# Six query and key chunks turned by VectorE and DMA instead of TensorE, in a float32 two-block transformer kernel

## The reference

```python
h = _rms_norm(x, attn_norm[l])
proj = h @ w_in                        # [256, 2048] @ [2048, 5664]
qf, kf, vf, ff, qn, kc, vc, ks, vs, kw, vw, gt = jnp.split(proj, cuts, axis=-1)
qf = _rms_norm(qf.reshape(B, T, Hf, Dh), fox_q_norm)      # 8 heads of 128
kf = _rms_norm(kf.reshape(B, T, Hf, Dh), fox_k_norm)      # 8 heads
qn = _rms_norm(qn.reshape(B, T, G, R, Dh), nsa_q_norm)    # 8 heads
# then: attention with a forget gate over qf, kf, vf (8 heads); compressed, selected and
# windowed attention over qn, kc/vc, ks/vs, kw/vw (8 heads, 2 groups); output projection;
# SwiGLU FFN.  The second block: adaLN, attention and a causal convolution, FFN.
```

## Time and profile before

| | |
|---|---|
| median of 3 runs | 2233.22 us (2232.3 to 2233.9) |
| the profiled execution | 2231.85 us |
| its span in the profile | 2230.1 us |
| TensorE (matmuls) busy | 2208.2 us, 99% |
| VectorE, ScalarE, GpSimd busy | 71%, 49%, 10% |
| DMA | 518.06 MB, mean 232 GB/s |

### The profile page before, as it was taken

One profiled execution on the slowest core, in us unless ns is written; L12 is line 12 of the kernel. 1 busy time (PEld: TensorE's weight loads), 2 busy tenths in 40 slices (PEclk: granted clock), 3 DMA queues, 4 the chain that ended last, 5 costly groups with the idle time before them and its releaser, 6 DMA issues.

```text
span 2230.1 us, 29184 instructions
## 1 busy us (share of the span) xinstructions
PE 2208.2 (99%) x10077; PEld 1826.6 (82%) x10077; DVE 1586.5 (71%) x2041; ACT 1096.5 (49%) x1536; POOL 232.5 (10%) x214
## 2 busy tenths in 40 slices
PE   9999999999999999999999999999999999999998
PEld 7888878888888888888888887788888888888886
DVE  7546678877777778877866888997887545554555
ACT  6556574544434444344455776654444344443444
POOL 5003001000000000000001887000010000000000
PEclk9999999999999999999999999999999999999999
DMA  8556628788888888888856664767997666666664
GB/s 293 169 183 190 195 76 309 263 290 284 285 288 288 285 282 283 289 289 281 272 163 194 192 182 130 260 247 244 307 294 252 196 200 203 202 191 195 199 203 146
DMA packets 310569, 518.06 MB, mean 232 GB/s; under 512 B 55320, under 2 KB 63896, under 8 KB 310192
## 3 DMA queue, kind: packets, MB, share of 16 engines
q1 hardware_dynamic: 306032, 515.73, 71.3%
q10 hardware_dynamic: 4416, 0.79, 0.2%
HBM read 510.15 MB, written 2.10 MB: 230 GB/s over the span
## 4 chain that ended last, share of the span: by engine, by line
PE 94%; DVE 2%; ACT 2%; issue 1%; DMA 1%; SPq 0%; DVEq 0%; ACTq 0%
PE bank L1111 31%; PE bank L1127 29%; PE bank L1128 29%; PE bank L1179 1%; PE bank L1096 1%; DVE w_both L2170 1%; PE bank L1082 1%; PE bank L1212 0%; ACT prob_mid L1653 0%; PE bank L1246 0%; PE bank L1200 0%; DMA raw<-in_w_in 0%; ACT w_both L1604 0%; DMA x_res<-in_x 0%; PE bank L1003 0%
## 5 line engine op out<-in xcount | busy, mean ns | idle before, releaser
L2170 DVE TENSOR_TENSOR w_both<-raw,w_both 128x1024 fp32r<-128x1024 f32 x763 | 950.8, 1250 | 520.2 <-ACT w_both L1604 508.4
L1604 ACT ACTIVATE w_both<-raw 128x1024 fp32r<-128x1024 f32 x763 | 806.4, 1060 | 969.1 <-PE bank L1111 920.4
L1127 PE MATMUL bank<-w_both,act_hi 128*128 128x512 f32 x1984 | 775.6, 391 | 1.7 <-ACT w_both L1604 1.7
L1128 PE MATMUL bank<-w_both,act_lo 128*128 128x512 f32 x1984 | 772.3, 389 | 0.0
L1111 PE MATMUL bank<-w_both,act_hi 128*128 128x512 f32 x2168 | 578.0, 390 | 1.1 <-ACT w_both L1604 0.6
L1111 PEld LDWEIGHTS bank<-w_both,act_hi 128*128 128x128 f32 x2168 | 405.7, 188 | 86.6 <-issue 1.8
L1127 PEld LDWEIGHTS bank<-w_both,act_hi 128*128 128x128 f32 x1984 | 372.5, 188 | 78.6 <-ACT w_both L1604 2.1
L1128 PEld LDWEIGHTS bank<-w_both,act_lo 128*128 128x128 f32 x1984 | 372.5, 188 | 76.1
L1127 PE MATMUL bank<-w_both,mid_hi 128*128 128x512 f32 x960 | 375.8, 391 | 1.1 <-DVE mid_lo L2081 0.4
L1128 PE MATMUL bank<-w_both,mid_lo 128*128 128x512 f32 x960 | 373.7, 389 | 0.0
L2128 DVE SCALAR_TENSOR_TENSOR ada_acc<-ada_raw,c_act,ada_acc 128x512 f32<-128x512 f32 x360 | 269.8, 749 | 10.9 <-DMA ada_raw<-in_ada_w 3.8
(11 more groups left out here) (315 smaller groups left out, 1027.9 us busy)
## 6 DMA issues: line engine op xcount, KB each, us to landing
ada_raw<-in_ada_w SPq DMA_DIRECT2D x192, 512.0 KB, 5.3
raw<-in_w_gate SPq DMA_DIRECT2D x176, 512.0 KB, 4.6
raw<-in_w_up SPq DMA_DIRECT2D x176, 512.0 KB, 4.8
raw<-in_w_down SPq DMA_DIRECT2D x176, 512.0 KB, 4.3
raw<-in_w_in SPq DMA_DIRECT2D x167, 512.0 KB, 3.6
raw<-in_w_out SPq DMA_DIRECT2D x60, 512.0 KB, 5.4
h_tok<-h_blk SPq DMA_DIRECT2D x128, 32.0 KB, 3.9
x_res<-in_x SPq DMA_DIRECT2D x8, 256.0 KB, 5.6
```

Source lines behind the costliest of these rows:

```text
L1127: pe.matmul(A_[t][:, :], h_, w_hi[:, s, kk, :], start=(k == 0), stop=False)
L1128: pe.matmul(A_[t][:, :], l_, w_hi[:, s, kk, :], start=False, stop=False)
L1604: act.activation(w_hi[:, U % SPLIT_SLOTS].rearrange("p k n -> p (k n)"), raw_of(c, u).rearrange("p k n -> p (k n)"), ACT.Copy).then_inc(hi ...
L2170: dve.tensor_tensor(w_lo[:, U % SPLIT_SLOTS].rearrange("p k n -> p (k n)"), raw_of(c, u).rearrange("p k n -> p (k n)"), w_hi[:, U % SPLIT_ ...
```

## The change

For six chunks (fq 0, fq 4, fk 0, fk 4, nq 0, nq 4) TensorE's transposes go. In their place:

- VectorE (`cut_heads`) turns `ysb` in 32x32 squares, two instructions of 128x512, in unit 3 of the next chunk behind `pre`. In chunks 1 and 7 (behind fq 0 and nq 0) it does so in unit 5. It counts `heads_cut` and `turned`.
- SyncE (`move_heads`) moves the squares with 16 DMAs of 32 KB, in four groups of four: the first behind the load of unit 7 of that chunk, after a wait for the cut, the others behind the loads of units 0, 1 and 2 of the chunk after. Each counts `heads_moved`.
- ScalarE and VectorE do `post` in unit 2 of the chunk after, not at the end of the chunk, and wait for `heads_moved`. They read the moved tile in SBUF and not the PSUM bank.

The tiles for squares lie over memory that is used at other times. The core of the diff:

```diff
+    CUT_TURNS = [("normed", "fq", 0), ("normed", "fq", 4), ("normed", "fk", 0), ("normed", "fk", 4),
+                  ("normed", "nq", 0), ("normed", "nq", 4)]
+    MOVED_IN = {c["C"] + 1: c["prev"] for c in S_IN1 + S_IN2 if c["prev"] in CUT_TURNS}
...
+            def move_heads(prev, a):
+
+                n, i = CUT_TURNS.index(prev), TURNS.index(prev)
+                blk, tok = squares_of(prev)
+                if a == 0:
+                    sp.wait_ge(heads_cut, n + 1)
+                    sp.wait_ge(turned, i + 1)
+                    sp.wait_ge(turn_out_a, i)
+                    sp.wait_ge(turn_out_d, i)
+                for q in range(4):
+                    sp.dma_start(tok[32 * q:32 * q + 32, :, :, :].rearrange("p t k (a j) -> p (t k) a j", a=4)[:, :, a, :],
+                                 blk[32 * a:32 * a + 32, :, :].rearrange("p t (k q j) -> p (t k) q j", q=4, j=32)[:, :, q, :]
+                                 ).then_inc(heads_moved, 16)
...
+                    if c["prev"] in CUT_TURNS and u == NU - 1:
+                        move_heads(c["prev"], 0)
+                    if c["C"] in MOVED_IN and u < 3:
+                        move_heads(MOVED_IN[c["C"]], u + 1)
...
+                if prev in CUT_TURNS:
                     return
                 i = TURNS.index(prev)
                 if prev[0] == "glu":
...
-                i = TURNS.index(prev)
-                act.wait_ge(turned, i + 1)
+                if prev in CUT_TURNS:
+                    act.wait_ge(heads_moved, 256 * (CUT_TURNS.index(prev) + 1))
+                else:
+                    act.wait_ge(turned, TURNS.index(prev) + 1)
...
+                    if u == 2 and c["C"] in MOVED_IN:
+                        post(MOVED_IN[c["C"]], None, None)
...
-                    if not c.get("blocks"):
+                    if not c.get("blocks") and c["prev"] not in CUT_TURNS:
                         post(c["prev"], c["C"], r)
...
+                    if c["prev"] in CUT_TURNS and u == (5 if c in S_IN1[1:2] + S_IN1[7:8] else 3):
+                        cut_heads(c["prev"], c["C"])
...
+            def cut_heads(prev, C):
+
+                n = CUT_TURNS.index(prev)
+                wait_read(dve, C - 1)
+                if prev == ("normed", "nq", 0):
+                    dve.wait_ge(blk_hi, 4)
+                if n >= 1:
+                    dve.wait_ge(heads_moved, 256 * n)
+                for t in range(TT):
+                    dve.transpose(squares_of(prev)[0][:, t, :], ysb[:, t, :]).then_inc((heads_cut, turned)[t], 1)
```

More of the change, by code:

```diff
@@ L380, in build_two_blocks @@
         begin = ExitStack()
+        filler("late_first", 8192, begin)
+        head_blk_b = sb("head_blk_b", [P, TT, CW], F32, begin)
+        begin.close()
+        begin = ExitStack()
+        filler("early_first", 4 * KD * T, begin)
+        head_blk_a = sb("head_blk_a", [P, TT, CW], F32, begin)
+        head_tok_a = sb("head_tok_a", [P, TT, HPC, P], F32, begin)
+        begin.close()
+        begin = ExitStack()
         filler("mid_first", 4 * KD * T, begin)
@@ L445, in build_two_blocks @@
         A = ExitStack()
-        heads = {n: sb(n, [P, k, T], F32, A) for n, k in
-                 (("fq", FOX_H), ("fk", FOX_H), ("nq", NSA_H), ("kc", NSA_G), ("vc", NSA_G), ("ks", NSA_G),
-                  ("kw", NSA_G))}
+        heads = {n: sb(n, [P, k, T], F32, A) for n, k in (("fq", FOX_H), ("fk", FOX_H), ("nq", NSA_H))}
+        A1 = ExitStack()
+        head_tok_b = sb("head_tok_b", [P, TT, HPC, P], F32, A1)
+        A1.close()
+        heads.update({n: sb(n, [P, NSA_G, T], F32, A) for n in ("kc", "vc", "ks", "kw")})
         vals = {n: sb(n, [P, TT, k, HD], F32, A) for n, k in (("fv", FOX_H), ("vs", NSA_G), ("vw", NSA_G))}
+        A1 = ExitStack()
+        A1.close()
         A1 = ExitStack()
@@ L490, in build_two_blocks @@
         a_keep = sb("a_keep", [P, TT, CW], F32, Cs)
+        head_tok_c = a_keep[:, :, :].rearrange("p t (k n) -> p t k n", n=P)
         uT = sb("uT", [P, CONV_G, CONV_K - 1 + T], F32, Cs)
@@ L553, in build_two_blocks @@
         mid_hi_done, mid_lo_done = sem("mid_hi_done"), sem("mid_lo_done")
+        heads_cut, heads_moved = sem("heads_cut"), sem("heads_moved")
         ada_loaded = [sem("ada_loaded0"), sem("ada_loaded1")]
@@ L616, in v @@
             def v(k0, k1):
+                if prev in CUT_TURNS:
+                    return squares_of(prev)[1][:, t, k0:k1, :]
                 return src[:, k0 * P:k1 * P].rearrange("p (k t) -> p k t", t=P)
@@ L632, in keep, with squares_of @@
                 put(heads[prev[1]][:, prev[2]:prev[2] + k, cols_t], v(0, k), gain).then_inc(done, 1)
+        def squares_of(prev):
+            if prev[1] in ("mq", "mk"):
+                return zsb, head_tok_c
+            return (head_blk_b, head_tok_b) if prev[1] == "nq" else (head_blk_a, head_tok_a)
         def adds_through(n):
@@ L1083, in consume @@
                         ins.then_inc(h_turned, 1)
+                    return
+                if prev in CUT_TURNS:
                     return
@@ L2085, in post @@
                     return
-                dve.wait_ge(turned, TURNS.index(prev) + 1)
+                if prev in CUT_TURNS:
+                    dve.wait_ge(heads_moved, 256 * (CUT_TURNS.index(prev) + 1))
+                else:
+                    dve.wait_ge(turned, TURNS.index(prev) + 1)
                 keep(dve, prev, 1, lambda o, s, g: dve.tensor_scalar(o, s, g, None, ALU.mult), turn_out_d)
```

## The result

The changed kernel takes 2245.41 us (median of 4 runs, 2245.03 to 2248.38), the kernel before, beside it, 2233.18 us (2232.3 to 2233.9). The ratio is 1.0059, 95% interval 1.0048 to 1.0071: slower by 12.2 us, where 8 were forecast with a range of 2231 to 2252. The profiled execution took 2245.03 us with a span of 2243.3, 13.2 above the one of before.

The account below looks back on a forecast made before the run. TensorE, busy 99% of the span, was taken to bound the kernel. Idle time of 6.0 + 0.7 + 4.6 + 2.0 = 13.3 us less 5.3 removed gave 8 us slower, a median of 2241.2 us, range 2231 to 2252.

Parts of the forecast that it names:

- The likeliest case: Late loads make TensorE idle 13.3 us against 5.3 us removed: 3 to 14 us slower; chance 0.61.
- Removed: TensorE's transposes in six chunks: six bursts of 0.89 us, 5.3 us off, the whole gain.
- VectorE's cut: Per chunk, two VectorE turns of 0.69 us each, 1.45 us with a handshake, between ysb and the next w_lo.
- A unit on SyncE: Four moves, a load and its gap on SyncE's queue: 3.0 us, more than TensorE's 2.72 us.
- Chunk 2: Behind fq 0: TensorE idles 6.0 us, 2.4 for w_hi and 1.6 for w_lo of unit 4 among it.
- Chunks 3 and 4: Chain from ysb to ysb takes 23.9 us against 21.8 for eight units, 25.6 in chunk 3: 0.7 us idle together.
- Chunk 8: Behind nq 0, cut after unit 5: 0.6 us before units 2 and 3, 2.4 + 1.6 at unit 4: 4.6 us idle.
- Chunk 9: Behind four short compression units, so little lead: three loads with moves between, 0 to 4 us idle, taken as 2.
- B: SyncE's issues grow when rings are full, to 0.8 us each; chunks 3 and 4 pay too: +14 to +30 us; chance 0.12.
- C: Stalls appear but shorter, loads landing at 3.5 us or less, chunk 9 keeping its lead: -3 to +3 us; chance 0.13.
- D: The lead absorbs everything and only the 5.3 us gain is left: 2227.9 us; chance 0.14.
- The rule on small pieces: Skill page: SBUF to SBUF copies don't pay for 128 B pieces; 16 moves 1.5 us, not 4.6; some 4 us slower.

Follow-up runs that it names:

- The four-move kernel: Changed kernel with one 128 KB move per group, four a chunk instead of sixteen, squares not exchanged between partitions: 2229.5 us, 0.9986 of the kernel before.
- The last kernel: Changed kernel with all sixteen moves a chunk started from GpSimd's queue and the copies behind unit 7 instead of unit 2: 2229.7 us, 0.9982 of the kernel before.

## Why the prediction came out as it did

**The likeliest case was right, and so was its mechanism.** TensorE bounds the kernel, SyncE was slower than TensorE for four units behind each cut, the loads of chunks 2 and 8 late by it, w_hi and then w_lo of unit 4 missing, chunks 5 to 7 and 10 free: all are in the rows, and the runs without moves, with four moves and with the starts on another queue show the cause. The size was short: 13.3 us of idle time forecast, 18.1 measured, with every chunk that stalled above its forecast. The median, 12.2 us slower, still lies in the likeliest case of +3 to +14, near its upper end.

**Step by step.**
- Removed, 5.3 us: 5.1 in the changed kernel. The kernel with the starts on GpSimd and late copies is 5.75 us ahead by chunk 10.
- VectorE's cut: no cost; the run without moves shows none. I had also written that SyncE's wait for the cut does cost. By itself it didn't: that run kept the wait, and chunk 2 had no idle time.
- A unit on SyncE, 3.0 us: 3.24. This is the term that was mis-sized. I took a load's start from the timeline of the second FFN, 0.47 us, where it began 0.18 us after the moves' end. Here it begins 0.05 us after (46.75 + 2.69 = 49.44, then 49.49), and takes 0.60. The kernel before shows 0.60 us too, at 1560.36, right behind the slow pair of the earlier trace rows, and I passed over it. The moves' starts were right (0.609 against 0.610).
- Landing of loads, 4.2 us: 4.3. Landing of the moves, 3.5: a median of 2.5; neither mattered.
- Chunk 2, 6.0 us: 6.7. The squares start near 64.4 (I had 63.4), as the loads come 3.24 apart; w_hi of unit 4 starts at 68.49, not 67.5. The split between w_hi and w_lo, 2.4 + 1.6, is 3.7 in all in the step of unit 4, and more came before units 0 to 3 (2.9 for 2.0).
- Chunks 3 and 4, 0.7: 2.5. The chain from one cut to the next was 23.9 by my sum and is 25.1 by the rows; four units on SyncE, each 0.24 longer than I took, are 1.0 of the 1.2. In chunk 3 that leaves half a microsecond of slack (25.6) where I had 1.7.
- Chunk 8, 4.6: 5.9, by the same units of 3.24. Chunk 9, 2 of 0 to 4: 3.0, inside its bounds; it wasn't taken apart further.
- Sum: 18.1 idle for 13.3. Less 5.1 it is 13.0, and the median moved by 12.2.

**The rivals.** B, growing starts, didn't come: the median stayed at 0.610 us, and the largest is 0.892 in fq and fk and 1.418 in nq. That starts grow with full rings, no run shows. C would have needed loads in 3.5 us or less and a chunk 9 that keeps its lead: the first four took 3.9 to 4.5 us, and chunk 9 idled 3.0. D, in which the lead absorbs everything, needed 0.35 us a start. The four-move kernel, at a quarter of the starts, comes near it; at the density of the changed kernel it took another queue. The rule on small pieces was weighed and set aside: with 1 KB pieces the DMA share falls by 0.07 and the idle time by 3 us of 18, so the pieces are a small part of the matter.

ScalarE's wait for the moved tiles I had put at nothing. In the changed kernel that is right (its first copy, at 61.95 us, starts without a wait), since the loads are later still; the wait became the next limit as soon as the loads were free.

## What to carry to other kernels

Count the starts on a queue as work of that queue: at 0.6 us each, four small transfers and a load are more than a 2.72 us unit of TensorE, though the DMA engines here were only 0.7 busy. Compare the sum with the pace of the engine that bounds, unit by unit, and not over a stage; then spread the transfers, merge them, or put them on a queue that is empty. When the queue is freed, look at once for who asks first for what the transfers bring, and move that request back.

## What the runs showed of the hardware that I had not expected

**How long SyncE takes to start a load depends on what stands right before it.** In the changed kernel, from 30 to 310 us, it is 0.37 us after a pause of 0.3 us or more, 0.47 us directly behind another load (0.467 to 0.476, twelve times) and 0.60 us directly behind a move (0.592 to 0.612, 22 times). The timeline in chunk 9 has the first and the last:

```profile
227.22 0.37 SPq L779 DMA_DIRECT2D raw<-in_w_in  x1
227.63 2.55 SPq L767 DMA_DIRECT2D head_tok_b<-head_blk_b  x4
230.24 0.59 SPq L779 DMA_DIRECT2D raw<-in_w_in  x1
```

**GpSimd starts the same moves as fast as SyncE**, 0.582 against 0.610 us, but they take longer to land, a median of 4.9 us (3.9 with the late copies) against 2.5. The quickest land alike, in 1.8 us from GpSimd and 1.9 from SyncE, and GpSimd's come sixteen in a row beside loads at full pace. The Trainium skill (DMA: Bandwidth & Descriptors, the section that compares SWDGE, GpSimd's way, and HWDGE, SyncE's) says that SyncE's way is set up faster; neither the starts nor the quickest landings show it here.

**The granted clock falls for some 3 us at a few places of this stage in some executions.** One is chunk 10, behind 32 short matmuls of 128x32; TensorE was busy all the time before. Windows of TensorE in the kernel with GpSimd's moves and late copies:

```profile
253.00:256.00 3.00, 3.00 (x29) 0.98 0.23 66
256.00:259.00 3.00, 3.00 (x8) 0.50 0.77 268
259.00:262.00 3.00, 3.00 (x14) 0.95 0.58 191
```

That is 1.2 GHz in the middle one. A matmul of 128x512 takes 0.63 us there and not 0.40, and unit 2 to 3 of chunk 10 takes 7.89 us, where the kernel before has 6.33 with the clock at 1.00: 1.6 us. It fell there in three more kernels (no moves; first cut early; five chunks with four moves a unit), and not in the other seven. The second place is chunk 1, from about 43 us, after a stall. It fell to 0.50 to 0.62 in four kernels, in which TensorE had been busy for 0.95, 0.41, 0.70 and 0.52 of the 2.0 us from 41 to 43 (four moves, none, two a unit, four a unit with five chunks); it stayed at 1.00 in the other seven (0.18 to 1.17, the kernel before 0.84, the changed one 0.56). The stall's length alone doesn't sort them. The third is behind the stall of chunk 8: 0.57 from 212 to 216 us in the first kernel with GpSimd's moves, and 0.58 and 0.57 from 214 to 218 us with 1 KB pieces and with the first cut early. The changed kernel, with the same stall, kept 1.00. Once it fell behind the stall of chunk 2 (0.50 from 71 to 74 us, five chunks with four moves a unit). A fall in chunk 1 or 10 costs about 1.6 us, as much as two bursts.

It is no property of a kernel alone. The three profiles without a fall have a mean clock of 0.999 over the whole execution, the eight with one or more 0.998 or less. Of 24 executions of the kernel before, 13 had 0.999 and took 2231.9 us on average, and ten had 0.998 and took 2233.5: 1.6 us more. The last kernel had 0.999 in three executions of eleven, with 2226.6 to 2226.8 us; the kernel before, beside it and at 0.999, took 2232.3. That is 5.6 us, what six bursts are worth (5.3), where the medians show 3.2. What decides whether the clock falls stays open: each kernel was profiled once, and no run was made for it.
